# Layer three's forget sums as one rounded operand, and the first step of the state space in another order

## The reference, cut to what matters

```python
def fox_attention(q, k, v, f_logit, q_gain, k_gain):
    q = rms_norm(q, q_gain)
    k = rms_norm(k, k_gain)
    c = jnp.cumsum(jax.nn.log_sigmoid(f_logit), axis=1)      # 512 x 8 heads
    ...
    s = jnp.einsum('bqhd,bkhd->bhqk', qi, k) * scale          # 8 heads of 64
    s = s + ci[..., None] - ck[:, :, None, :]                 # forget sums
    s = jnp.where(kpos[None, :] <= pi[:, None], s, NEG_INF)
    pr = jax.nn.softmax(s, axis=-1)
    return jnp.einsum('bhqk,bkhd->bqhd', pr, v)
```

## Time and profile before

| | |
|---|---|
| Median of 3 runs | 2821.59 us (2819.82 to 2824.32) |
| The profiled execution's own time | 2821.0 us |
| Its span in the trace | 2819.3 us |
| PE busy, share of the span | 2553.6 us, 91% |
| DVE, ACT, POOL busy | 1790.0, 963.6, 1462.8 us |
| First layer's attention, first scores to last head turned | about 188 to 277 us |
| Layer three's attention | about 1551 to 1670 us |
| S5: VectorE's norm to the last state | about 2152 to 2293 us |

### The profile page before, as it was taken

One profiled execution on the slowest core, in us unless ns is written; L12 is line 12 of the kernel. 1 busy time (PEld: TensorE's weight loads), 2 busy tenths in 40 slices (PEclk: granted clock), 3 DMA queues, 4 the chain that ended last, 5 costly groups with the idle time before them and its releaser, 6 DMA issues.

```text
span 2819.3 us, 36780 instructions
## 1 busy us (share of the span) xinstructions
PE 2553.6 (91%) x12750; PEld 2002.6 (71%) x12750; DVE 1790.0 (63%) x2191; ACT 963.6 (34%) x1494; POOL 1462.8 (52%) x1234
## 2 busy tenths in 40 slices
PE   4978989969999998999498989999995889999998
PEld 3754777847777777788386358888884768888887
DVE  6769866757777776667688556666135954666324
ACT  2013267723443432677312323222013632222102
POOL 4730334435544553344465016666777837666775
PEclk8977889979999998999799689999997999999999
DMA  8745479942233223798432113333231123333222
GB/s 311 255 144 204 176 260 329 325 152 84 81 99 96 85 80 107 279 342 300 134 79 79 56 45 96 99 93 98 97 116 45 38 53 90 104 89 104 88 92 82
DMA packets 319122, 386.73 MB, mean 137 GB/s; under 512 B 51578, under 2 KB 259214, under 8 KB 318902
## 3 DMA queue, kind: packets, MB, share of 16 engines
q1 hardware_dynamic: 261424, 335.84, 36.3%
q10 hardware_dynamic: 34438, 28.08, 3.3%
q0 software_dynamic: 23168, 21.59, 2.3%
HBM read 397.62 MB, written 55.41 MB: 161 GB/s over the span
## 4 chain that ended last, share of the span: by engine, by line
PE 36%; POOL 20%; issue 19%; DVE 13%; DMA 9%; ACT 2%; SPq 0%; ACTq 0%; POOLq 0%; DVEq 0%
POOL WL L836 14%; PE PAIR L528 6%; PE PAIR L529 5%; PE PAIR L530 5%; POOL WH L832 5%; PE PAIR L1840 4%; PE BANK L528 2%; PE BANK L529 2%; PE BANK L530 2%; PE PAIR L1810 2%; PE BANK L2279 2%; DMA RAW<-in_ffn_w_up 2%; DMA RAW<-in_moe_w 2%; DVE ADA_SUM L633 1%; DVE ADA_SUM L631 1%
## 5 line engine op out<-in xcount | busy, mean ns | idle before, releaser
L836 POOL TENSOR_TENSOR WL<-RAW,WH 128x512 fp32r<-128x512 f32 x584 | 819.2, 1432 | 12.2
L528 PE MATMUL PAIR<-HH,WH 128*128 128x512 f32 x1792 | 712.4, 398 | 50.4 <-POOL HL L1125 28.8
L529 PE MATMUL PAIR<-HL,WH 128*128 128x512 f32 x1792 | 703.1, 392 | 0.0
L530 PE MATMUL PAIR<-HH,WL 128*128 128x512 f32 x1792 | 701.9, 392 | 0.0
L831 POOL TENSOR_TENSOR TURN<-ONES 128x1 f32<-128x1 f32 x146 | 33.7, 231 | 932.0 <-PE PAIR L530 854.5
L528 PEld LDWEIGHTS PAIR<-HH,WH 128*128 128x128 f32 x1792 | 339.6, 190 | 134.1 <-issue 46.1
L530 PEld LDWEIGHTS PAIR<-HH,WL 128*128 128x128 f32 x1792 | 339.7, 190 | 72.1
L529 PEld LDWEIGHTS PAIR<-HL,WH 128*128 128x128 f32 x1792 | 339.9, 190 | 71.4 <-issue 2.4
L832 POOL TENSOR_SCALAR WH<-RAW 128x2048 fp32r<-128x2048 f32 x146 | 282.3, 1934 | 0.0
L2014 POOL DMA_INDIRECT XG<-htok_scratch,GATHER_I x78 | 106.2, 1362 | 259.2 <-PE PAIR L1810 147.7
L528 PE MATMUL BANK<-WH,GH 128*128 128x256 f32 x624 | 180.7, 290 | 0.0
(11 more groups left out here) (525 smaller groups left out, 4883.8 us busy)
## 6 DMA issues: line engine op xcount, KB each, us to landing
RAW<-in_moe_w SPq DMA_DIRECT2D x156, 512.0 KB, 7.0
RAW<-in_ffn_w_up SPq DMA_DIRECT2D x88, 512.0 KB, 4.6
W2RAW<-in_moe_w SPq DMA_DIRECT2D x78, 512.0 KB, 5.9
ADA_B<-in_ada_w SPq DMA_DIRECT2D x30, 1024.0 KB, 5.5
RAW<-in_ssm_w_in SPq DMA_DIRECT2D x48, 512.0 KB, 4.8
ADA_A<-in_ada_w SPq DMA_DIRECT2D x18, 1024.0 KB, 7.8
RAW<-in_ffn_w_down SPq DMA_DIRECT2D x32, 512.0 KB, 3.9
RAW<-in_ev_w_in SPq DMA_DIRECT2D x20, 512.0 KB, 4.8
```

What stands on the lines that cost most here:

```text
L528: nc.tensor.matmul(o, wh, xh, start=start, stop=False)
L529: nc.tensor.matmul(o, wh, xl, start=False, stop=False)
L530: return nc.tensor.matmul(o, wl, xh, start=False, stop=stop)
L836: ins = pool.tensor_tensor(WL[:, s, c], RAW[:, s, c], WH[:, s, c].bitcast(F32), ALU.subtract)
```

## The change

1. The forget sums become a rounded operand FCUT on 128 partitions: zero, but rows 0 to 7 and 64 to 71 hold the sums rounded to fp32r and rows 32 to 39 and 96 to 103 what the rounding left. MINUS_HEAD becomes fp32r on 128 partitions, with its 8 rows at 0, 32, 64 and 96. The product of L1337 now takes 64 rows of each, at the same partitions as the head's K and Q, and is one rounded product.
2. MINUS_HEAD is made at the end of `dve_moe(dve, 1)` in five instructions, not at the head of `dve_evin` in one.
3. In `dve_evin` FCUT is zeroed, the sums are scanned in place, copied twice and subtracted twice.
4. S5's first step: the norm signals after its first tile too; POOL does W1_PR and PRP of step 0 before the constants and does no longer wait for the pairs before them; ScalarE and PE take step 0 in the order W1X, turned, CAX, U4, kernel, and only then the layouts of step 1. POOL splits the first two units of glu after its steps 2 and 3.

```diff
-    FCUM = sb("FCUM", [HEADS, 2, SEQ], F32, r)
-    MINUS_HEAD = sb("MINUS_HEAD", [HEADS, HEADS, P], F32, r)
+    FCUM = sb("FCUM", [HEADS, SEQ], F32, r)
+    FCUT = sb("FCUT", [P, SEQ], F32R, r)
+    MINUS_HEAD = sb("MINUS_HEAD", [P, HEADS, P], F32R, r)
...
-            ins.then_inc(h_ready, 1)
-            dve.passed(h_ready, 1)
+                if k in (0, KD - 1):
+                    ins.then_inc(h_ready, 1)
+            dve.passed(h_ready, 2)
...
-                        ins = nc.tensor.matmul(bank[:, at:at + wide], MINUS_HEAD[:, h, :], FCUM[:, 1, 0:wide],
+                        ins = nc.tensor.matmul(bank[:, at:at + wide], MINUS_HEAD[a:a + HD, h, :], FCUT[a:a + HD, 0:wide],
...
+    def dve_minus_head(dve):
+        dve.link(dve.e.tensor_scalar(MINUS_HEAD[:], bcast(ONES[:, 0:HEADS], 2, P), 0.0, None, ALU.mult))
+        for at in (0, 32, 64, 96):
+            dve.e.tensor_scalar(MINUS_HEAD[at:at + HEADS], bcast(IDENT[0:HEADS, 0:HEADS], 2, P), -HD ** 0.5, None, ALU.mult)
...
         else:
+            dve_minus_head(dve)
             dve_s5_angles(dve)
...
-        dve.e.tensor_scalar(MINUS_HEAD[:], bcast(IDENT[0:HEADS, 0:HEADS], 2, P), -HD ** 0.5, None, ALU.mult)
...
-        dve.e.tensor_copy(FCUM[:, 0, :], full_bank(dve, b)[0:HEADS, :]).then_inc(bank_free[b % 4], 1)
+        dve.link(dve.e.tensor_scalar(FCUT[:], LATER[:], 0.0, None, ALU.mult))
+        total = FCUM[:]
+        dve.e.tensor_copy(total, full_bank(dve, b)[0:HEADS, :]).then_inc(bank_free[b % 4], 1)
         dve.e.wait_ge(bank_free[b % 4], b // 4 + 1)
-        dve.e.tensor_tensor_scan(FCUM[:, 1, :], ONES[0:HEADS, 0:1].broadcast_to([HEADS, SEQ]), FCUM[:, 0, :], 0.0,
-                                 ALU.mult, ALU.add).then_inc(w["cum_ready"], 1)
+        dve.link(dve.e.tensor_tensor_scan(total, ONES[0:HEADS, 0:1].broadcast_to([HEADS, SEQ]), total, 0.0, ALU.mult, ALU.add))
+        dve.e.tensor_copy(FCUT[HD:HD + HEADS], total)
+        dve.link(dve.e.tensor_copy(FCUT[0:HEADS], total))
+        for at in (32, HD + 32):
+            ins = dve.e.tensor_tensor(FCUT[at:at + HEADS], total, FCUT[0:HEADS].bitcast(F32), ALU.subtract)
+        ins.then_inc(w["cum_ready"], 1)
...
     def pool_s5(pool):
+        w = s5_sems
+        pool.wait(w["reloaded"], 16)
+        pool.link(pool.e.memset(W1X[:], 0.0))
+        pool_s5_inputs(pool, 0)
+        for b in range(plan.b["s5c"], plan.b["s5c"] + 4):
+            pool.e.wait_ge(bank_free[b % 4], b // 4 + 1)
+        pool.link(pool.e.memset(CAX[:], 0.0))
+        pool_s5_outputs(pool, 0)
         pool_s5_consts(pool)
-
-        for k in range(KD):
-            pool_s5_step(pool, k)
...
+        for k in range(1, KD):
+            pool_s5_inputs(pool, k)
+            pool_s5_outputs(pool, k)
+            if k in (2, 3):
+                split_unit(pool.e, plan.u["glu"] + k - 2)
...
+        if k == 0:
+            pe_s5_turned(pe, 0)
+        if k < 2:
+            pe.wait(h_ready)
+        pe_s5_u_rows(pe, k)
+        if k:
+            pe_s5_turned(pe, k)
...
     def act_s5(act):
         w = s5_sems
+        act_s5_w1_blocks(act, 0)
+        act_s5_turned(act, 0)
         act.wait(w["consts"])
-
+        act_s5_ca_blocks(act, 0)
+        act_s5_u_rows(act, 0)
         act_s5_decay(act, 0)
-        act_s5_blocks(act, 0)
-        act_s5_blocks(act, 1)
-        act_s5_inputs(act, 0)
         act_s5_kernel(act, 0)
+        act_s5_w1_blocks(act, 1)
+        act_s5_ca_blocks(act, 1)
...
-        split_units(pool.e, plan.u["glu"], plan.unit)
+        split_units(pool.e, plan.u["glu"] + 2, plan.unit)
```

More of the change, by code:

```diff
@@ L3194, in step_at, with s5_a @@
         return slice(k, k + 1) if e is None else bass.ds(e * 2 + k, 1)
-    def s5_a(k, i):
+    def s5_a(k, name):
+        i = ("u", "w0", "w1", "kernel").index(name) if k else ("w0", "w1", "u", "kernel").index(name)
         return plan.b["s5"] + (4 + 6 * (k - 1) + i if k else i)
@@ L3223, in pool_s5_consts @@
         pool.e.memset(FIRST[:, 0:1], 0.0)
-        pool.e.memset(W1X[:], 0.0)
-        pool.e.memset(CAX[:], 0.0)
         pool.e.memset(W3[:], 0.0).then_inc(w["consts"], 1)
         pool.wait(w["consts"])
-        for b in range(plan.b["s5c"], plan.b["s5c"] + 4):
-            pool.e.wait_ge(bank_free[b % 4], b // 4 + 1)
-        pool.wait(w["reloaded"], 16)
     def dve_s5_turning(dve, k):
@@ L3296, in pe_s5_prepare, with pe_s5_turned @@
         ins.then_inc(bank_ready, 1)
+    def pe_s5_turned(pe, k):
+        w, par = s5_sems, k % 2
         pe.wait(w["w1x"])
         for part in range(2):
-            bank = take_bank(pe, s5_a(k, 1 + part))
+            bank = take_bank(pe, s5_a(k, f"w{part}"))
             for i in range(4):
@@ L3302, in pe_s5_prepare @@
             ins.then_inc(bank_ready, 1)
+    def pe_s5_prepare(pe, k):
+        w, par = s5_sems, k % 2
+        if k == 0:
[5 more added lines that the diff above has]
+            pe_s5_turned(pe, k)
         pair = take_pair(pe, plan.p["s5"] + k)
-        for i in (0, 1, 2):
-            b = s5_a(k, i)
+        for name in ("u", "w0", "w1"):
+            b = s5_a(k, name)
             pe.e.wait_ge(bank_free[b % 4], b // 4 + 1)
@@ L3314, in pe_s5_prepare @@
         pe.wait(w["skip"])
-        bank = take_bank(pe, s5_a(k, 3))
+        bank = take_bank(pe, s5_a(k, "kernel"))
         for i in range(4):
@@ L3356, in pe_s5 @@
     def pe_s5(pe):
-        pe.wait(h_ready)
         pe_s5_prepare(pe, 0)
@@ L3363, in pe_s5, with act_s5_u_rows, act_s5_turned, act_s5_w1_blocks @@
             pe_s5_output(pe, None, k)
-    def act_s5_inputs(act, k):
-        par = k % 2
+    def act_s5_u_rows(act, k):
+        par, b = k % 2, s5_a(k, "u")
         if k >= 2:
             act.e.wait_ge(bank_ready, s5_y(k - 2) + 1)
-        b = s5_a(k, 0)
         act.e.activation(U4[:, par].rearrange("p t n -> p (t n)"), full_bank(act, b)[:], ACT.Copy).then_inc(bank_free[b % 4], 1)
+    def act_s5_turned(act, k):
+        par = k % 2
         for part in range(2):
-            b = s5_a(k, 1 + part)
+            b = s5_a(k, f"w{part}")
             bank = full_bank(act, b)
             act.e.activation(W1_T[:, par, part].rearrange("p t n -> p (t n)"), bank[:], ACT.Copy).then_inc(bank_free[b % 4], 1)
-    def act_s5_blocks(act, k):
+    def act_s5_w1_blocks(act, k):
         w, par = s5_sems, k % 2
@@ L3381, in act_s5_blocks @@
         if k >= 2:
-            act.e.wait_ge(bank_ready, s5_a(k - 2, 3) + 1)
+            act.e.wait_ge(bank_ready, s5_a(k - 2, "kernel") + 1)
         for part in range(2):
@@ L3411, in act_s5_kernel @@
     def act_s5_kernel(act, k):
-        par, b = k % 2, s5_a(k, 3)
+        par, b = k % 2, s5_a(k, "kernel")
         kernel = full_bank(act, b)[0:32, :].rearrange("p (t n) -> p t n", n=P)
```

17 lines of the change are left out of this document (11 added, 6 removed).

## The result

The changed kernel takes 2791.1 us (2788.6 to 2791.6, four executions) where the kernel before took 2822.1 beside it: a ratio of 0.989, 95% interval 0.988 to 0.990. The forecast was 2794. Measured a second time, the changed kernel gave 2792.4 and 0.9897 (0.9879 to 0.9914). The profiled execution has a span of 2789.7 us against 2819.3.

A forecast was written before the change was run, and what follows sets the result against it. PE, busy 91% of the span, was taken to bound layer three's attention, with VectorE nearly bounding the first layer's. Terms -22.5 + 3.2 + 0.5 - 9 = -27.8 us from 2821.0 gave 2793.2, median 2794; range 2783 to 2809.

The forecast's parts named there:

- The attention: Layer three's attention: cheaper scores shorten PE's work until VectorE nearly sets the pace; 22.5 us won, bounds 8 and 28.
- Head 0's period: Attention, first period after the first turning: PE's 17.25 us loses the scores' 4.6 and becomes 12.6.
- The five periods: Attention, the periods after head 0's, to 1655.23: 10.4 us each instead of 12.3, 9.6 us saved.
- The rival that the clock takes the gain: Attention: PE stays at the lower clock level, five periods of 13.3 us, gain 8, total 2808 us; chance 0.13.
- The rival that VectorE's floor is reached: Attention: upper clock in all heads, 28 us won there, 33 to 37 in total, 2786 us; chance 0.08.
- The price of a product: Attention, a head's scores on PE: 6.3 us against 10.9 at the lower clock level, 3.3 against 5.9 at the upper.
- the slower rival: Attention: each of 64 turns between fp32 and rounded products empties the array; at 0.6 us a turn, 2831 us; chance 0.03.
- the product is no cheaper: Attention: the rounded product costs what fp32 did, only S5's gain stays, 2816 us; chance 0.03.
- The forget sums: VectorE's added zeroing, copies and subtractions before the attention: 3.2 us lost, all on PE's start; bounds 2.0 and 6.
- The end of the experts: Five MINUS_HEAD instructions in VectorE's idle time, 6.0 us if undisturbed: 0.5 us lost, bounds 0 and 2.5.
- S5: First step of S5: VectorE's 14.81 us wait for its first input shrinks; 9 us won, bounds 1 and 14.
- the signs: Expected in the profile: PE's 8.29 us wait about 11, VectorE's L2666 2 to 4 later, VectorE over 85% busy in attention.

The follow-up runs named there:

- the three traces with the old attention: The kernel before (2820 to 2825 us) and two measurements of the changed kernel with all but its S5 edits taken back (2815.5 and 2814.7 us).
- the tables cut: Changed kernel with only two of VectorE's six table instructions per head kept in layer three's attention, so the tables hold wrong numbers: 2782.9 us, ratio 0.986.
- the attention alone: Changed kernel without its S5 edits, S5 being as in the kernel before: 2805.0 us, ratio 0.995; measured again 2806.5 us, 0.993.
- both runs with the sums behind the norm: Changed kernel, FCUT zeroed at the experts' end, scan, casts and subtractions behind the gMLP norm: 2785.9 us; the same with fp32 forget product from head 3: 2790.7 us.

## Why the prediction was right, point by point

**The attention (22.5 forecast, 26.8 measured).** From the first score to evout it is 119.6 before and 92.8 after. The first two heads: 8.3 forecast, 8.75 measured. Head 0's period: 4.6, and 4.8. The five periods: 9.6, and 13.3 and 12.7 in the two traces. The last two heads: nothing, as forecast. (Against the mean of the three traces with the old attention, 117.8, and of the two of the changed kernel it is 24.8, of which the five periods are 11.3.) The mechanism was the one forecast, PE's scores until VectorE sets the pace, and mainly the size of the third term was off: I had taken 10.4 us for a period, between the first layer and VectorE's floor of 9.2, and it came out at 9.7, because four of the five, in the second trace three, ran at the upper level (granted 0.78 against 0.70 before). The rival that the clock takes the gain is refuted in its full form, but each period at the lower level still costs 10.3 to 12.5 us against 8.5 to 9.8. The page that spoke for it (the Trainium skill, TensorE: Matmul & The Clock Gate), by which the throttled state is the default and activity releases it, didn't help to say which periods fall: PE fell back at 1608.89 behind a wait of 2.42 us, but the kernel before has no gap from 1577 to 1656 and a granted clock of 0.70, and with the tables cut PE works 32.9 of the five periods' 41.0 us, waits 1.62 in each, and has 1.00. The rival that VectorE's floor is reached (0.08) came near as well: its 28 us is the better number for the 26.8 of this pair of traces, the forecast's 22.5 for the 24.8 of the means.

**The price of a product.** 6.3 us for a head's scores was forecast, 5.73 came. My reading of the gap as loads that are not hidden when 8 rows follow 64 was right in kind and wrong in size: not 0.1 us for each record but 0.29 for each turn, in either direction. Two of its numbers hid that. The 5.1 us of K and Q alone hold short gaps between products (the two heads of that stretch take 5.6 and 4.6; without gaps it is 4.57 from the first start to the outputs'), and the 5.0 of the forget product's columns were counted from rows that already hold the turns (1280 fp32 columns are 4.27 at 1.71 for 512). The same holds for the sentence on the slower rival, that 0.1 us is the most that a turn can cost: the turns of the kernel before cost three times that. Turns between fp32 and rounded cost next to nothing (K and Q alone take 4.57 us a head, with the rounded products 5.73, 1.16 more, of which 1280 columns at 1.2 GHz are 1.07: 0.1 us for all seven), so that the rival falls, as does the one that the product is no cheaper.

**The forget sums (3.2 forecast, 6.9 measured).** This is the step that failed: its upper bound of 6 didn't hold. From the last TAB_NEW to the end of the norm's mean VectorE is 10.45 us later, of which 3.57 were there before. Zeroing was 1.5 us, the casts 0.84 for two, but the two subtractions 4.1 instead of 1.3, and VSQ behind them 1.0 longer (the last instruction of the mean, 0.17 instead of 0.81, gave some back). All of it lay on PE's start, as said. I had let "all stretched" mean 1.4 times, the mean of S5; here two short instructions each waited for a long one of POOL. The Trainium skill (SBUF — State Buffer, Who interferes with whom) has this case: an instruction of VectorE with two inputs in SBUF contends with one of GpSimd that reads SBUF, and who comes second is blocked for the whole of the other. The traces agree closely. Both subtractions came second and took 2.41 and 1.66 us beside POOL's 1.89 and 1.57, against 0.68 alone; in the attention alone the first began 0.03 us before POOL's instruction and took 0.68, POOL's 2.41 instead of 1.89, and the second, then behind it, 2.28. The zeroing was disturbed too: it took 1.51 us beside POOL's WL, 0.42 where POOL was idle (both runs with the sums behind the norm).

**The end of the experts (0.5 forecast, 0 measured).** The five instructions took 3.5 us, not 6.0 (0.69 each), in a gap of VectorE that still ended with a wait of 1.23 for PE. One scatter of POOL beside them took 1.34 instead of 0.97, the last one its 0.97, and nobody waited for it.

**S5 (9 forecast, 10 measured).** The wait of 14.8 us is gone. The layer before was disturbed for 2.5 us (1.5 forecast) and HF for 0.5; from the first states to the last it is 1.9 longer (4.3 forecast: 3 of contention, 1.3 for a late second step, which didn't come late). 14.8-2.5-0.5-1.9 = 9.9. The 9 us that the prediction worked out from the page's rule, by which S5 would have given 1.5, didn't come, but the rule itself holds instruction by instruction: each of the six additions to the sum of squares came second and ended only behind the POOL instruction under way. They lost 0.4 us each, 2.5 in all, because POOL's were short and partly over (the one shown begins at 2126.55 beside one that ends at 2127.06); the 9 us had each wait for a whole one.

**Sum.** -26.8+6.9+0-10.0 = -29.9, against the -27.8 forecast and -29.6 in the span. Two errors, 4.3 too little in the attention (2.3 by the means) and 3.7 too little lost at the forget sums, nearly cancelled: that the total came within 3 us is in part luck. Of the signs, PE's wait (15.0, not 11) and the start of the norm (6.5 later, not 2 to 4) missed with the forget sums; VectorE was busy 83% in the attention, just under the 85%.

## What to carry to other kernels

A product that contracts few rows between products that contract 64 pays at every turn; bring it to their row count first, with zeros if need be, and only then ask what a cheaper format gives: here the rows gave 18 to 20 of 24 to 27 us. Price what is added on an engine ahead of a wait by what the other engine on the shared path does at that moment, instruction by instruction and in which order they begin, not by a mean, and look at once for a gap behind the wait: the same work there cost PE nothing, and that version (the forget sums behind the norm, 2785.9 us, ratio 0.987) is the fastest one of this study that computes the whole. Where an engine's queue is reordered so that one consumer is served earlier, look how much it has to spare for the last of its consumers: POOL had 0.5 us, and starting it later cost the kernel 8 to 9.

## What the hardware showed that I had not expected

A turn between 8 and 64 contracted rows costs 0.29 us at the lower level of the clock and 0.20 at the upper, whatever the width. Across a turn the load of the stationary operand begins only with its product; without one it begins a record ahead. A turn between fp32 and the rounded format costs 0.1 us for seven. An 8x512 subtraction takes 0.68 us undisturbed, as a 128x512 one does, and beside POOL's split it ended 0.5 us behind the instruction of POOL that had begun before it: 2.41, 2.28 or 1.66 us, by what was left of that one; begun first, it took its 0.68 and POOL's was the longer one. With the rounded product one or two of the attention's five periods, not always the same ones, ran at the lower level of the clock from trace to trace, and the five together took from 47.2 to 51.3 us with the same work in them.
